# First gathers in the routing block, a held pair of weight loads, and a software pipeline over the overflow units of a mixture-of-experts layer

## The reference

```python
lg = h @ w_rg + b_rg                       # 4 groups
g_sel, p_grp = argmax(lg), max(softmax(lg))
le = (h @ w_re + b_re)[group g_sel]        # 8 experts of the group
top_v, top_i = top_k(le, 2)
w_top = softmax(top_v) * p_grp
# for both experts e of a token, with weight w:
hid = silu(h @ w_e1[e]) * (h @ w_e3[e])    # 1024 -> 256
y  += w * (hid @ w_e2[e])                  # 256 -> 1024
```

## Time and profile before

| | |
|---|---|
| median of 3 runs | 1605.72 us |
| lowest, highest | 1603.92, 1609.12 us |
| the profiled execution | 1603.87 us |
| its span in the profile | 1601.9 us |
| mean granted clock of TensorE, share of full speed | 0.926 |
| busy in the span: PE, DVE, ACT, POOL | 85%, 36%, 17%, 7% |
| moved by DMA | 242.36 MB |

### The profile page before, as it was taken

The page is one execution under the profiler, slowest core; times in us unless marked ns, Lnnn a source line. Parts: engine busy times, 40 slices in busy tenths (PEclk is TensorE's granted clock), DMA queues, the critical chain, the costliest instruction groups (busy, mean ns, idle before and its releaser), DMA issues. The chain is left out here.

```text
span 1601.9 us, 16015 instructions
## 1 busy us (share of the span) xinstructions
PE 1364.6 (85%) x6201; PEld 805.5 (50%) x6201; DVE 579.8 (36%) x1294; ACT 279.7 (17%) x574; POOL 106.9 (7%) x150
## 2 busy tenths in 40 slices
PE   4999995978967999899999999999948888786864
PEld 2655553555635889466777555554543333232321
DVE  4231568223381345244444411115751111110108
ACT  2102441034102433211111100000111101110110
POOL 0000003011000000000000000002011111110100
PEclk9799997989987999999999999999958999998987
DMA  9332322310301101022111127103068999999923
GB/s 374 145 131 106 105 76 82 130 55 1 82 14 32 34 6 58 0 80 66 40 40 40 40 79 246 63 20 141 40 284 325 421 424 423 424 423 373 391 85 151
DMA packets 57742, 242.36 MB, mean 151 GB/s; under 512 B 21668, under 2 KB 30436, under 8 KB 42820
## 3 DMA queue, kind: packets, MB, share of 16 engines
q1 hardware_dynamic: 51476, 229.79, 37.3%
q0 software_dynamic: 6048, 10.50, 1.7%
q10 hardware_dynamic: 144, 1.05, 0.2%
HBM read 233.54 MB, written 19.31 MB: 158 GB/s over the span
## 5 line engine op out<-in xcount | busy, mean ns | idle before, releaser
L464 PE MATMUL bank<-hT,ring 128*128 128x512 f32 x384 | 202.5, 609 | 0.0
L2431 PE MATMUL bank<-ew,xgT 128*64 128x512 f32 x672 | 162.8, 640 | 35.0 <-DMA ew<-in_experts 18.4
L1531 PE MATMUL bank<-hT,w_ab 128*128 128x512 f32 x256 | 131.1, 594 | 0.8 <-issue 0.8
L2431 PEld LDWEIGHTS bank<-ew,xgT 128*64 128x64 f32 x672 | 57.6, 148 | 136.0 <-issue 136.0
L465 PEld LDWEIGHTS bank<-hT,ring 128*128 128x128 f32 x384 | 74.2, 193 | 94.4 <-issue 94.4
L2445 PE MATMUL bank<-ew,hidT 128*64 128x512 f32 x336 | 80.1, 619 | 12.8 <-issue 12.3
L1532 PEld LDWEIGHTS bank<-hT,w_ab 128*128 128x128 f32 x256 | 48.6, 190 | 61.2 <-issue 61.2
L2540 DVE SCALAR_TENSOR_TENSOR uh<-uh,bank 128x256 f32<-128x256 f32 x21 | 8.8, 421 | 191.6 <-ACT uh L2494 191.6
L465 PE MATMUL bank<-hT,ring 128*128 128x128 f32 x384 | 74.6, 276 | 0.0
L1942 PE MATMUL bank<-w_out,mT 128*128 128x512 f32 x160 | 70.9, 604 | 2.2 <-PEq L1464 2.2
L867 PE MATMUL bank<-hT,ring 128*128 128x512 f32 x128 | 66.0, 597 | 0.0
(11 more groups left out here) (427 smaller groups left out, 2102.6 us busy)
## 6 DMA issues: line engine op xcount, KB each, us to landing
ew<-in_experts SPq DMA_DIRECT2D x41, 2048.0 KB, 20.8
ew<-in_experts SPq DMA_DIRECT2D x41, 1024.0 KB, 22.5
ring<-in_blocks SPq DMA_DIRECT2D x10, 2048.0 KB, 9.5
mhalf<-in_mods SPq DMA_DIRECT2D x16, 1024.0 KB, 5.0
w_ab<-in_merge SPq DMA_DIRECT2D x16, 768.0 KB, 4.4
mstage<-in_mods SPq DMA_DIRECT2D x3, 2048.0 KB, 18.6
w_c<-in_merge SPq DMA_DIRECT2D x8, 768.0 KB, 4.4
yt<-expert_rows SPq DMA_DIRECT2D x5, 1024.0 KB, 9.0
```

What stands on the lines that cost most here:

```text
L464: pe.matmul(lat[:, :], w, hT[:, k, P:T], start=(k == 0), stop=(k == KD - 1))
L1531: pe.matmul(bank[5][:, :], w[:, k, :], hT[:, k, P:T], start=(k == 0), stop=(k == KD - 1))
L2431: mm = pe.matmul(bank[2 + x % 2][hs, :], xgT[:, x % 2, k, hs], ew1[:, 2 * (x % 2) + h, 2 * DE * k:2 * DE * (k + 1)], start=(k == 0), stop= ...
```

## The change

1. In the routing block GpSimd waits for `idx` and issues the gathers of units 0 to 3 there, with the indices straight from `idx`. In the experts block these units' `prepare` only copies `gate`.
2. SyncE holds the two second-layer pieces of unit 1 in the routing block until unit 0's gather has landed.
3. SyncE's overflow loads go by unit: both first-layer pieces when ffn1 of the unit two back is done, then both second-layer pieces when its ffn2 is done.
4. The overflow's compute takes the order of the other units: on TensorE the transposes of unit n + 1 stand between first layer and hidden transposes of n, on ScalarE and VectorE the copies of n + 1 between their work on n, each under its own condition (`ahead`). TensorE waits for the second half's first-layer weights before ffn1 and for its second-layer weights before hT_ and ffn2.

```diff
             for n in range(2):
                 for h in range(2):
                     load_first(sp, A["experts"][2 * n + h], 2 * n + h)
+                if n:
+                    sp.wait_ge(gathered[0], 16)
                 for h in range(2):
                     load_second(sp, A["experts"][2 * n + h], 2 * n + h)
...
+            last_row.extend([pool.to_reg(T - 1), pool.to_reg(2 * T - 1)])
             pool.memset(xg[:], 0.0).then_inc(zeroed, 1)
+            pool.wait_ge(zeroed, 1)
+            pool.wait_ge(v9.sem, v9.after("idx"))
+            for x in range(4):
+                pool.indirect_dma_start(xg[:, x, :], None, h2d, bass.IndirectOffsetOnAxis(idx[:, 0, x:x + 1], 0),
+                                        bounds_check=last_row[0], oob_is_err=False).then_inc(gathered[x], 16)
...
-        for u in range(NXH):
-            n, s = NP + u // 2, 2 * (u // 2 % 2) + u % 2
-            with sp.If(units > u):
-                sp.wait_ge(pt_m.sem["f1"], n - 2 + 1)
-                expert = sp.value_load(extra[0:1, 1 + u:2 + u], min_val=0, max_val=NE - 1)
-                load_first(sp, EXPERT(expert), s)
-                sp.wait_ge(pt_m.sem["f2"], n - 2 + 1)
-                load_second(sp, EXPERT(expert), s)
+        for n in range(NP, NU):
+            u, s = 2 * (n - NP), 2 * (n % 2)
+            for load, before in ((load_first, "f1"), (load_second, "f2")):
+                for h in range(2):
+                    with sp.If(units > u + h):
+                        if h == 0:
+                            sp.wait_ge(pt_m.sem[before], n - 2 + 1)
+                        expert = sp.value_load(extra[0:1, 1 + u + h:2 + u + h], min_val=0, max_val=NE - 1)
+                        load(sp, EXPERT(expert), s + h)
...
-            if not (isinstance(n, int) and n < 4):
-
-                pool.wait_ge(pt_m.sem["xT"], n - 4 + 1)
-                pool.wait_ge(ve_m.sem["hid"], n - 4 + 1)
+            if isinstance(n, int) and n < 4:
+                pool.tensor_copy(gsc[:, x, :], gate[:, n:n + 1]).then_inc(po_m.sem["small"], 1)
+                return
+            pool.wait_ge(pt_m.sem["xT"], n - 4 + 1)
+            pool.wait_ge(ve_m.sem["hid"], n - 4 + 1)
...
+        def ahead(n):
+            if n < NU:
+                with pe.If(units > 2 * (n - NP)):
+                    xT(n, n % 4)
+                    pe.nop()
+
+        ffn1(NP - 1, 3)
+        ahead(NP)
+        hT_(NP - 1, 3)
+        ffn2(NP - 1, 3)
         for n in range(NP, NU):
-            with pe.If(units > 2 * (n - NP) + 1):
-                weights_ready(got_w13, n, n, 2)
-                weights_ready(got_w2, n, n, 2)
+            u, odd = 2 * (n - NP), 2 * (n % 2) + 1
+            with pe.If(units > u + 1):
+                pe.wait_ge(got_w13[odd], half16(n, n % 2))
                 pe.nop()
-            with pe.If(units > 2 * (n - NP)):
-                xT(n, n % 4)
+            with pe.If(units > u):
                 ffn1(n, n % 4, 1)
+                pe.nop()
+            ahead(n + 1)
+            with pe.If(units > u + 1):
+                pe.wait_ge(got_w2[odd], half16(n, n % 2))
+                pe.nop()
+            with pe.If(units > u):
                 hT_(n, n % 4)
                 ffn2(n, n % 4, 1)
                 pe.nop()
```

More of the change, by code:

```diff
@@ L2104, in program @@
     zeroed = nc.alloc_semaphore("gather_zeroed")
+    gathered = [nc.alloc_semaphore(f"gathered{i}") for i in range(4)]
+    last_row = []
     G_MAX, G_MIN, G_SUM, G_P, T_M1, T_M2, T_N1, T_N2, T_E, T_S, W_1, W_2, _ = range(13)
@@ L2306, in program @@
     gsc = sb("gsc", [P, 4, 1])
-    gathered = [nc.alloc_semaphore(f"gathered{i}") for i in range(4)]
     scattered = [nc.alloc_semaphore(f"scattered{i}") for i in range(4)]
@@ L2333, in sync_units @@
         units = sp.value_load(extra[0:1, 0:1], min_val=0, max_val=NXH)
-        for u in range(NXH):
-            n, s = NP + u // 2, 2 * (u // 2 % 2) + u % 2
-            with sp.If(units > u):
-                sp.wait_ge(pt_m.sem["f1"], n - 2 + 1)
-                expert = sp.value_load(extra[0:1, 1 + u:2 + u], min_val=0, max_val=NE - 1)
-                load_first(sp, EXPERT(expert), s)
-                sp.wait_ge(pt_m.sem["f2"], n - 2 + 1)
-                load_second(sp, EXPERT(expert), s)
-    last_row = []
+        for n in range(NP, NU):
[7 more added lines that the diff above has]
+                        load(sp, EXPERT(expert), s + h)
     def pool_units(pool):
         def prepare(n, x):
-            if not (isinstance(n, int) and n < 4):
-                pool.wait_ge(pt_m.sem["xT"], n - 4 + 1)
-                pool.wait_ge(ve_m.sem["hid"], n - 4 + 1)
+            if isinstance(n, int) and n < 4:
[3 more added lines that the diff above has]
+            pool.wait_ge(ve_m.sem["hid"], n - 4 + 1)
             pool.tensor_copy(ig[:, x, :], idx[:, 0, bass.ds(n, 1)])
@@ L2447, in ffn2, with step @@
             mm.then_inc(pt_m.sem["f2"], 1)
-        def step(n, x, more=True):
+        def step(n, x):
             ffn1(n, x)
-            if more:
-                xT(n + 1, (x + 1) % 4)
+            xT(n + 1, (x + 1) % 4)
             hT_(n, x)
@@ L2461, in pe_units @@
                 step(4 * i + (4 + x), x)
-        for x in range(4):
-            step(NP - 4 + x, x, more=(x < 3))
+        for x in range(3):
+            step(NP - 4 + x, x)
         units = pe.value_load(extra[0:1, 0:1], min_val=0, max_val=NXH)
+        def ahead(n):
[7 more added lines that the diff above has]
+        ffn2(NP - 1, 3)
         for n in range(NP, NU):
-            with pe.If(units > 2 * (n - NP) + 1):
-                weights_ready(got_w13, n, n, 2)
-                weights_ready(got_w2, n, n, 2)
+            u, odd = 2 * (n - NP), 2 * (n % 2) + 1
+            with pe.If(units > u + 1):
+                pe.wait_ge(got_w13[odd], half16(n, n % 2))
                 pe.nop()
-            with pe.If(units > 2 * (n - NP)):
-                xT(n, n % 4)
+            with pe.If(units > u):
                 ffn1(n, n % 4, 1)
+                pe.nop()
[4 more added lines that the diff above has]
+            with pe.If(units > u):
                 hT_(n, n % 4)
@@ L2501, in y_, with step @@
             act.activation(yo[:, x, 0:512], bank[5][:, :], ACT.Copy).then_inc(ac_m.sem["y"], 1)
-        def step(n, x, more=True):
+        def step(n, x):
             tanh(n, x)
-            if more:
-                x_(n + 1, (x + 1) % 4)
+            x_(n + 1, (x + 1) % 4)
             h_(n, x)
@@ L2515, in act_units, with ahead @@
                 step(4 * i + (4 + x), x)
-        for x in range(4):
-            step(NP - 4 + x, x, more=(x < 3))
+        for x in range(3):
+            step(NP - 4 + x, x)
         units = act.value_load(extra[0:1, 0:1], min_val=0, max_val=NXH)
+        def ahead(n):
+            if n < NU:
+                with act.If(units > 2 * (n - NP)):
+                    x_(n, n % 4)
+                    act.nop()
+        tanh(NP - 1, 3)
+        ahead(NP)
+        h_(NP - 1, 3)
+        y_(NP - 1, 3)
         for n in range(NP, NU):
             with act.If(units > 2 * (n - NP)):
-                x_(n, n % 4)
                 tanh(n, n % 4)
+                act.nop()
+            ahead(n + 1)
+            with act.If(units > 2 * (n - NP)):
                 h_(n, n % 4)
@@ L2564, in dve_units, with ahead @@
                 step(4 * i + (4 + x), x)
-        for x in range(4):
-            step(NP - 4 + x, x, more=(x < 3))
+        for x in range(3):
+            step(NP - 4 + x, x)
         units = dve.value_load(extra[0:1, 0:1], min_val=0, max_val=NXH)
+        def ahead(n):
+            if n < NU:
+                with dve.If(units > 2 * (n - NP)):
+                    x_(n, n % 4)
+                    dve.nop()
+        hid_(NP - 1, 3)
+        ahead(NP)
+        y_(NP - 1, 3)
         for n in range(NP, NU):
             with dve.If(units > 2 * (n - NP)):
-                x_(n, n % 4)
                 hid_(n, n % 4)
+                dve.nop()
+            ahead(n + 1)
+            with dve.If(units > 2 * (n - NP)):
                 y_(n, n % 4)
@@ L2589, in _ @@
         def _(pool):
-            last_row.extend([pool.to_reg(T - 1), pool.to_reg(2 * T - 1)])
-            pool.wait_ge(zeroed, 1)
             pool_units(pool)
```

## The result

The changed kernel's median is 1594.3 us over five runs (1591.13 to 1596.65), the kernel before 1605.62 over five; the ratio is 0.9912 with a 95% interval of 0.9884 to 0.994. The forecast was 1591.2, range 1586 to 1597. The profiled execution took 1591.13 us for a span of 1589.3, 12.6 less than before.

A forecast was written before the change was run, and what follows sets the result against it. The weight stream was taken to bound the experts until the overflow, where TensorE's own chain set the time. Overflow 14.4 us, minus 0.8 for the clock, plus 0.0 at the start gave 13.6: 1591.2 us, range 1586 to 1597.

The forecast's parts named there:

- The overflow: Units 16 to 20: the last second layer ends at 1536.1 instead of 1550.47, 14.4 us gained (12.0 to 16.6).
- 0.8 for the clock: Units 19 and 20: a first layer slowed by the lower clock after a wait, half the time, minus 0.8 us.
- The period D: Overflow: time per unit at the weight stream's pace, taken as 15.7 us, between 14.9 and 16.6.
- The start: Routing to unit 0: earlier gather issue offset by the hold, net 0.0 us, from 1.4 gain to 1.4 loss.
- The cost of the hold: Before TensorE's first transpose: a pair of load issues, 0.98 us, and a block change, 0.35 us.
- rival 3: Start: gathers had only waited behind weights, so with the hold TensorE starts 2.9 us earlier, 1589.2 us; chance 0.08.
- The final block: End of the kernel: starts 5.3 us after the last second layer's matmul and doesn't change.
- Rival 1: Overflow: the scatter-gather chain rules, 3.0 us gained (1602.7) or slower (1610.5); chance 0.05 no change, 0.03 slower.
- S: Overflow: time from a scatter's issue until GpSimd goes on, 10.0 us.
- the margin of 3 us in two units: Overflow: scatter-gather chain of 26.5 to 28.5 us for two units, under the weight stream's 31.4, so hidden.
- Rivals 2 and 4: 2: late gather, 3.7 us lost, chance 0.06; 4: overflow weights at 18 to 19 us, 6 to 8 gained, 0.05.
- The branches: Overflow: more conditional blocks, five instead of two per unit on TensorE; the empty units' cost only above 0.2 us each.

The follow-up runs named there:

- e6: The kernel before with only the overflow's compute in the new order, loads and start as before: 1595.03 us in one run.
- e5: The kernel before with only SyncE's overflow loads in the new order, start and compute as before: 1606.97 us in one run.
- e9: The changed kernel with the held pair moved to the experts block, no wait for each overflow scatter, seven extra matmuls: 1588.63 us, ratio 0.9886.
- e10: The changed kernel with the held pair moved to the experts block and no wait for each overflow scatter: 1588.63 us, ratio 0.9881.
- e11: The changed kernel run again with the same code, against the kernel before: 1596.95 us, ratio 0.9932.

## Why the prediction was right, and where it was off

- **What bounds.** Right. Unit 0's first layer starts the weight stream, 230 us long in every kernel up to unit 15, and then TensorE's own chain ruled. Changing the chain (e6) brought 7.8 of the 10.3 us by which the stretch fell, and changing the loads alone (e5) none. The 16.4 us a unit that the prediction read off the serial chain held some lower clock; unit 19, at the upper one, took 15.2.
- **The overflow: forecast 14.4, less 0.8 for the clock; measured 10.3 in the same stretch.** Three terms of the sum were off. Unit 16 was to start 0.3 us behind unit 15's second layer and started 2.7 behind (unit 15's layers themselves were 1.7 us shorter, at the upper clock, and the pieces came 0.7 us later): 2.4. The period D was 16.1 instead of 15.7: 48.3 us for three instead of 46.9, 1.4. Unit 20's first layer started 13.5 us after unit 19's instead of 13.1, by the wait for its transposes' gather: 0.4. Together 4.2, and 73.5 + 4.2 is the 77.6 measured, to 0.1. The loss at the lower clock fell on unit 17, not on 19 or 20, and was hidden by the wait for weights, so the 0.8 was not needed. That was luck of this execution: in e9, e10 and e11 unit 20's second layer took 5.35 us.
- **The start: forecast 0.0; measured 1.0 at unit 0's first layer in this pair, 2.2 on average over the traces.** The cost of the hold was right: 1.3 us from the held pair's issue to the transposes. The gather's own time was the mis-sized term, 5.9 instead of 8.4: this is rival 3 (given 0.08), which came, 2.5 us at the transposes where it had 2.9; the clock then took 1.5 back in this pair (0.4 on average), which the prediction did not have at this place. So two terms that it lacked partly cancelled in the profiled pair.
- **The final block** was taken as unchanged and took 1.6 us more in this pair, by a clock that rose later. With 46.5 us in another execution of the same code, the forecast of no change stands. And that the profiled span fell by 12.6, near the forecast of 13.6, is in part chance: 1.2 us ahead of the first weight issue and 1.7 of unit 15's clock helped, 1.6 of the final block's went against it.
- **Rival 1** (scatter-gather chain), given 0.08, did not set the pace in the changed kernel's profiled execution, but came near it. S was 13.1 and 13.8 us instead of 10.0, which I had taken from one scatter with no gather right ahead of it, and the gather behind the first of them took 10.9 instead of 8 to 10. From the end of unit 16's second layer to that of unit 18's the chain took 32.5 us, not 26.5 to 28.5, so the margin of 3 us in two units was gone. In the changed kernel's profiled execution it cost 0.4 us, since behind the wait of 1.22 TensorE waited for weights anyway; in e11_change_again the waits cost some 2, beside the clock.
- **Rivals 2 and 4** did not come. The branches cost nothing that is seen: TensorE has no gap named issue above 0.8 us after unit 15, and the final block still follows 5.3 us after the last matmul.

## What to carry to other kernels

Before a wait chain through DMAs is called hidden, price it with the spread of landings and in the new order of issues, not with one landing of the old order: scatters that now came 2 to 3 us behind a gather took 14 us where the one that had been read took 10. A wait for a landing belongs behind a block's end, not ahead of it, where all engines pay for it. And a reordering of loads pays only after the compute asks for them early: compute first, then loads. Last, before an effect of 2 us is read off one pair of traces, see how far two traces of the same code lie apart: here 6 us from unit 15 on, most of it the clock.

## What the runs showed of the hardware

A gather of one unit took 4.2 to 5.9 us while the weight queue ran empty and 8.7 to 12.0 us with it full, the same code otherwise. Under a full stream a scatter took 13.8 to 14.8 us when it was issued 2.1 to 2.9 us behind a gather, and 10.6 at 8.5 us behind one. The granted clock rose to its upper level 5.7 to 8.7 us after the first transposes, 35.5 to 39.9 us after the first weight issue, in twelve executions; with seven extra matmuls in the wait it was up when the transposes began. The same kernel took 90.9 us from unit 15 on in one execution and 97.2 in another, some 1.7 us of it from a wait for a gather and the rest from the clock.
